# Strassen pairs in the first feed-forward as in the second, with both start-ups reordered

## What is computed

```python
x = rms_norm(x, final_norm_w)                                   # end of the first block: x's own norm
x = x + 0.5 * swiglu_ffn(rmsnorm(x, ffn1_norm), ffn1_w_in, ffn1_w_down)
...
mem_n = rmsnorm(mem, mem_norm)                                  # the memory's norm
x = x + 0.5 * swiglu_ffn(rmsnorm(x, ffn2_norm), ffn2_w_in, ffn2_w_down)

def swiglu_ffn(x, w_in, w_down):
    a, b = jnp.split(x @ w_in, 2, axis=-1)                      # w_in is 1024 x 5632
    return (jax.nn.silu(a) * b) @ w_down                        # w_down is 2816 x 1024
```

## Time and profile before

| | |
|---|---|
| median of 3 runs | 2434.7 us (2434.04 to 2436.02) |
| the profiled execution's own time | 2434.53 us |
| its span | 2432.8 us |
| PE busy | 2409.9 us, 99% of the span |
| DVE, ACT, POOL busy | 1243.0, 1095.1, 1314.3 us |
| granted TensorE clock, mean of the span | 0.997 of full speed |
| DMA | 92 GB/s mean |
| chain that ended last | PE 90%, DVE 7%, ACT 2% |

### The profile page before, as it was taken

The page is one execution under the profiler, slowest core; times in us unless marked ns, Lnnn a source line. Parts: engine busy times, 40 slices in busy tenths (PEclk is TensorE's granted clock), DMA queues, the critical chain, the costliest instruction groups (busy, mean ns, idle before and its releaser), DMA issues.

```text
span 2432.8 us, 33977 instructions
## 1 busy us (share of the span) xinstructions
PE 2409.9 (99%) x13114; PEld 2014.6 (83%) x13114; DVE 1243.0 (51%) x2325; ACT 1095.1 (45%) x1686; POOL 1314.3 (54%) x1722
## 2 busy tenths in 40 slices
PE   9999999999999999999999999999999999899998
PEld 6887788888788787888888888878988788899987
DVE  7965765322796586432332113199366433766502
ACT  5444676323534467532443323242366523566521
POOL 5553544555564455455555554585443455777753
PEclk9999999999999999999999999999999999999999
DMA  4232221222222212222322232332222222233322
GB/s 150 91 120 77 70 78 66 99 96 96 86 96 75 87 61 79 78 96 96 113 96 96 97 101 89 128 117 78 79 85 71 70 95 95 87 105 105 105 96 87
DMA packets 64412, 224.45 MB, mean 92 GB/s; under 512 B 7367, under 2 KB 10951, under 8 KB 64124
## 3 DMA queue, kind: packets, MB, share of 16 engines
q1 hardware_dynamic: 62620, 216.49, 26.7%
q0 software_dynamic: 1632, 5.78, 0.8%
HBM read 219.57 MB, written 3.99 MB: 92 GB/s over the span
## 4 chain that ended last, share of the span: by engine, by line
PE 90%; DVE 7%; ACT 2%; issue 0%; DMA 0%; SPq 0%; DVEq 0%; ACTq 0%
PE proj L193 69%; PE proj L2144 5%; PE att L2144 3%; PE att L193 2%; PE proj L914 1%; PE att L893 1%; PE att L1005 1%; PE att L904 1%; PE att L992 1%; PE att L2344 1%; PE att L947 1%; PE att L936 1%; DVE h_low L551 1%; ACT b_logits L2793 1%; DVE dk L1466 0%; DVE probs L1497 0%
## 5 line engine op out<-in xcount | busy, mean ns | idle before, releaser
L170 POOL TENSOR_TENSOR weight_low<-ring,weight_high 128x256 fp32r<-128x256 f32 x1432 | 1120.5, 814 | 1002.9 <-ACT weight_high L140 980.5
L193 PE MATMUL proj<-h_high,weight_high 128*128 128x512 f32 x1648 | 647.9, 393 | 1.6 <-POOL weight_low L170 1.5
L193 PE MATMUL proj<-h_low,weight_high 128*128 128x512 f32 x1648 | 641.7, 389 | 0.0
L193 PE MATMUL proj<-h_high,weight_low 128*128 128x512 f32 x1648 | 641.6, 389 | 0.0
L140 ACT ACTIVATE weight_high<-ring 128x1024 fp32r<-128x1024 f32 x353 | 371.7, 1054 | 354.6 <-PE proj L193 323.0
L193 PEld LDWEIGHTS proj<-h_high,weight_high 128*128 128x128 f32 x1648 | 309.4, 188 | 71.3 <-issue 5.1
L193 PEld LDWEIGHTS proj<-h_low,weight_high 128*128 128x128 f32 x1648 | 309.3, 188 | 65.1
L193 PEld LDWEIGHTS proj<-h_high,weight_low 128*128 128x128 f32 x1648 | 309.5, 188 | 62.4
L193 PE MATMUL proj<-b_act_high,weight_high 128*128 128x512 f32 (+1 forms) x352 | 135.0, 383 | 0.0
L193 PE MATMUL proj<-b_act_high,weight_low 128*128 128x512 f32 (+1 forms) x352 | 134.7, 383 | 0.0
L193 PE MATMUL proj<-b_act_low,weight_high 128*128 128x512 f32 (+1 forms) x320 | 122.6, 383 | 0.0
(11 more groups left out here) (623 smaller groups left out, 4711.2 us busy)
## 6 DMA issues: line engine op xcount, KB each, us to landing
ring<-in_stream SPq DMA_DIRECT2D x398, 512.0 KB, 3.4
xT<-in_x SPq DMA_DIRECT2D x4, 512.0 KB, 6.9
idx<-gate_rows POOLq DMA_DIRECT2D x8, 256.0 KB, 4.2
out<-hT SPq DMA_DIRECT2D x8, 256.0 KB, 2.2
bias_rows<-bias_row SPq DMA_DIRECT2D x2, 512.0 KB
b_logits<-in_mem POOLq DMA_DIRECT2D x1, 1024.0 KB, 8.1
bias_rows<-bias_row SPq DMA_DIRECT2D x1, 768.0 KB
consts<-in_const SPq DMA_DIRECT2D x1, 576.0 KB, 10.4
```

Of the source, the lines that this page charges most:

```text
L170: self.s_low.on(pool.tensor_tensor(self.low[:, c % self.slots, cols], self.raw[:, c % self.slots, cols], self.high[:, c % HIGH, cols], ALU ...
L193: mm = pe.matmul(out, a, b, start=(k == 0 and i == 0), stop=(k == n - 1 and i == 2))
```

## The change

- `ffn1` is paired as `ffn2` is. Its leads are a0, b0, a1, b1; its steps 2 to 21 are pairs. The dense step, its silu, gating and splits are gone.
- In both, the norm's sum stands before the lead's sixth slice (k = 5, was k = 6), and its spread before the eighth (k = 7, was at b0's first).
- Both start-ups (from the spread to the end of pair 0) are reordered on DVE and ACT. The weight forms of pair 0 go to other banks (`form_banks`), so that they need not wait for the leads to be emptied. T2's raw form has a place of its own, which lets T2's low part go ahead of T4. T4's high part and a1's silu go behind the snapshots of pair 0. ACT's first two form highs change places. In pair 0 DVE makes the forms of pair 1 behind two of its corners.
- x's own norm is spread over the pairs: two squares in each of pairs 2 to 5, the sum on PE before pair 7 (in a bank of its own), the root in pair 7, half of the reciprocal in each of pairs 8 and 9, one tile scaled in each of pairs 10 to 17.
- The memory is loaded when the last pair's T1 corner is done; its squares follow on ACT in d0, and its sum and norm come behind d1 (was d0). `power_rows`, 64 small matmuls, moves from behind d3 to behind d5.

The diff, cut to its core:

```diff
 NORMS = ["0", "1", "ffn1", "mix", "ffn2", "fin2"]
-SPLIT_NORMS = NORMS[:4]
-PAIRED = ["f2"]
+SPLIT_NORMS = ["0", "1", "mix"]
+PAIRED, PAIRED_NORMS = ["f1", "f2"], ["ffn1", "ffn2"]
...
-    total, spread = ((2, 0), (2, 2)) if n == NORMS[0] else ((0, KD - 2), (1, 0))
+    total, spread = ((2, 0), (2, 2)) if n == NORMS[0] else ((0, 5), (0, 7)) if n in PAIRED_NORMS else ((0, KD - 2), (1, 0))
...
+X_TOTAL = 7
+X_SQUARES = {j: (2 * j - 4, 2 * j - 3) for j in range(2, 6)}
+X_INVERSE = {8: slice(0, HALF), 9: slice(HALF, T)}
+X_SCALE = 10
 HIGH_AT = {0: [], 1: [0, 1], 2: [2, 3], NP: [KF - 1]}
...
-        if n in PAIRED:
-            g += [(f"{n}a1", OWN), (f"{n}b1", OWN)] + [(f"{n}p{i}", OWN) for i in range(2, KF)]
-        for i in range(1, KF if n not in PAIRED else 1):
-            g += [(f"{n}a{i}", "a" if i > 1 else OWN), (f"{n}b{i}", "v")]
-            if n == "f1" and i == 7:
-                g += [("ms_x", "a")]
-        g += [(f"{n}d0", "v")] + between + [(f"{n}d{d}", "v") for d in range(1, KD)]
+        g = [(f"ms_{n}", "a")] + [(f"{n}{x}{i}", OWN) for i in range(2) for x in "ab"]
+        for j in range(NP):
+            g += [("ms_x", OWN)] if n == "f1" and j == X_TOTAL else []
+            g += [(f"{n}p{j + 2}", OWN)]
...
+    def form_banks(n, j):
+
+        return (att[4], att[5], pair_alpha(n, 1)) if j == 0 else att[0:3]
     def s_slot(z):
...
             for j in range(NP):
+                if n == "f1" and j == X_TOTAL:
+                    G.open(pe, "ms_x")
+                    pe.wait_ge(s_xsum.sem, 1)
...
                     continue
                 product(f"{n}d{d}", xs, ready)
-                if n == "f1" and d == 0:
+                if n == "f1" and d == 1:
                     memory_sum()
-                if n == "f1" and d == 3:
+                if n == "f1" and d == 5:
                     power_rows()
...
+        def memory():
+
+            W.round(act, "f1d0")
+            act.wait_ge(s_mem.sem, 16)
+            for k in range(KD):
+                s_msq.on(act.activation(memsq[:, k, :], memT[:, k, :], ACT.Square))
...
+            act.wait_ge(s_sf.sem, s_sf.base + 2 * q_ + 1)
+            W.used(act, cb - HIGH)
+            s_sh.on(act.activation(W.high[:, cb % HIGH, 0:T], b1[:, :], ACT.Copy))
             act.wait_ge(s_sf.sem, s_sf.base + 2 * q_ + 2)
             s_slot_free(act, 3 * q_)
-            s_sh.on(act.activation(s_slot(3 * q_)[0], att[1][:, :], ACT.Copy))
-            W.used(act, cb - HIGH)
-            s_sh.on(act.activation(W.high[:, cb % HIGH, 0:T], att[0][:, :], ACT.Copy))
+            s_sh.on(act.activation(s_slot(3 * q_)[0], b2[:, :], ACT.Copy))
             act.wait_ge(s_sf3.sem, s_sf3.base + 2 * q_ + 2)
             s_sh.on(act.activation(s_slot(3 * q_ + 1)[0], s_slot(3 * q_ + 1)[2], ACT.Copy))
...
             at = KD * NORMS.index(norm)
             act.wait_ge(S.s_h.sem, at + 4)
-            x_high_part("11")
-            act.wait_ge(s_tf.sem, s_tf.base + 1)
-            x_high_part("T1")
-            W.round_one(act)
+            x_high_part(n, "11")
+            act.wait_ge(s_tf.sem, formed + 1)
+            x_high_part(n, "T1")
             act.wait_ge(S.s_h.sem, at + KD)
             norm_copy(S, act, norm)
-            x_high_part("21")
+            x_high_part(n, "21")
+            act.wait_ge(s_tf.sem, formed + 2)
+            x_high_part(n, "T2")
+            W.round_one(act)
             act.preload_act_table_set("silu_and_others")
-            act.wait_ge(s_tf.sem, s_tf.base + 2)
-            x_high_part("T2")
             act.wait_ge(s_lead.sem, base + 1)
             s_silu.on(act.activation(act_raw(0), act_raw(0), ACT.Silu))
-            x_high_part("22")
             form_highs(n, 0)
-            act.wait_ge(s_tf.sem, s_tf.base + 4)
-            x_high_part("T3")
-            act.wait_ge(s_lead.sem, base + 3)
-            s_silu.on(act.activation(act_raw(1), act_raw(1), ACT.Silu))
-            G.whole(act, f"{n}b1")
-            x_high_part("T4")
+            x_high_part(n, "22")
+            act.wait_ge(s_tf.sem, formed + 3)
+            x_high_part(n, "T3")
             for j in range(NP):
                 if j + 1 < NP:
                     W.round_one(act)
                 snapshots(n, j, lambda: gate_highs(j))
+                if j == 0:
+                    act.wait_ge(s_tf.sem, formed + 4)
+                    G.whole(act, f"{n}b1")
+                    x_high_part(n, "T4")
+                    act.wait_ge(s_lead.sem, base + 3)
+                    s_silu.on(act.activation(act_raw(1), act_raw(1), ACT.Silu))
+                if n == "f1" and j in X_SQUARES:
+                    for k in X_SQUARES[j]:
+                        s_xsq.on(act.activation(x_squares[:, k, :], xT[:, k, :], ACT.Square))
+                if n == "f1" and j == X_TOTAL:
+                    G.whole(act, "ms_x")
...
-            s_sf.on(dve.tensor_tensor(att[1][:, :], att[0][:, :], a[:, 0:T], ALU.subtract))
+            s_sf.on(dve.tensor_tensor(b2[:, :], b1[:, :], a[:, 0:T], ALU.subtract))
             settle(dve, s_sf)
-            s_sf.on(dve.tensor_tensor(att[2][:, :], a[:, T:UNIT], att[1][:, :], ALU.subtract))
+            s_sf.on(dve.tensor_tensor(b4[:, :], a[:, T:UNIT], b2[:, :], ALU.subtract))
...
+            s_tf.on(dve.tensor_tensor(x_form(n, "T1"), x_form(n, "12"), x_form(n, "11"), ALU.subtract))
             for k in range(4, KD):
                 scaled(k)
             settle(dve, s_tf)
             settle(dve, S.s_h)
-            s_tf.on(dve.tensor_tensor(T_raw["T2"], B_raw["22"], T_raw["T1"], ALU.subtract))
+            s_tf.on(dve.tensor_tensor(x_form(n, "T2"), x_form(n, "22"), x_form(n, "T1"), ALU.subtract))
+            t_low("T1")
             dve.wait_ge(S.s_copied.sem, copied)
             G.whole(dve, f"{n}a0")
             s_lead.on(dve.tensor_tensor(act_raw(0), att[0][:, :], rstd[:], ALU.mult))
+            weight_forms(n, 0)
+            form_low(n, 0, 0)
+            t_low("T2")
+            form_low(n, 0, 1)
+            s_tf.on(dve.tensor_tensor(x_form(n, "T3"), x_form(n, "22"), x_form(n, "12"), ALU.subtract))
             G.whole(dve, f"{n}b0")
             link(dve.tensor_tensor(att[1][:, :], att[1][:, :], rstd[:], ALU.mult))
-            t_low("T1")
-            dve.wait_ge(s_silu.sem, base // 3 * 2 + 1)
+            t_low("T3")
+            form_low(n, 0, 2)
+            dve.wait_ge(s_xpl.sem, s_xpl.base + 12 * f + 4)
+            s_tf.on(dve.tensor_tensor(x_form(n, "T4"), x_form(n, "21"), x_form(n, "T2"), ALU.subtract))
+            dve.wait_ge(s_silu.sem, 2 * f + 1)
             s_lead.on(dve.tensor_tensor(act_raw(0), att[1][:, :], act_raw(0), ALU.mult))
+            t_low("T4")
             G.whole(dve, f"{n}a1")
             s_lead.on(dve.tensor_tensor(act_raw(1), att[2][:, :], rstd[:], ALU.mult))
-            settle(dve, s_lead)
-            weight_forms(n, 0)
-            form_low(n, 0, 0)
-            dve.wait_ge(s_xpl.sem, s_xpl.base + 4)
-            settle(dve, s_tf)
-            s_tf.on(dve.tensor_tensor(T_raw["T4"], B_raw["21"], T_raw["T2"], ALU.subtract))
-            t_low("T2")
-            form_low(n, 0, 1)
-            s_tf.on(dve.tensor_tensor(T_raw["T3"], B_raw["22"], B12, ALU.subtract))
-            t_low("T3")
-            form_low(n, 0, 2)
-            t_low("T4")
             for j in range(NP):
                 more = j + 1 < NP
                 if j >= 1:
...
                 gate_lows(j)
+                if n == "f1":
+                    own_norm(j)
+                if j == 0:
+                    corner(n, j, 0)
+                    corner(n, j, 1)
+                    weight_forms(n, j + 1)
+                    corner(n, j, 2)
+                    for m in range(3):
+                        form_low(n, j + 1, m)
+                    continue
...
+        def own_norm(j):
+
+            for k in X_SQUARES.get(j - 1, ()):
+                dve.wait_ge(s_xsq.sem, k + 1)
+                if k >= 1:
+                    ins = dve.tensor_tensor(x_rstd, x_squares[:, 0, :] if k == 1 else x_rstd, x_squares[:, k, :], ALU.add)
+                    if k < KD - 1:
+                        link(ins)
+                    else:
+                        s_xsum.on(ins)
+            if j in X_INVERSE:
+                dve.wait_ge(s_xroot.sem, s_xroot.base + 1)
+                link(dve.reciprocal(x_rstd[:, X_INVERSE[j]], x_rstd[:, X_INVERSE[j]]))
+            k = j - X_SCALE
+            if 0 <= k < KD:
+                s_xscale.on(dve.scalar_tensor_tensor(xT[:, k, :], xT[:, k, :], vec("fin1", k), x_rstd, ALU.mult, ALU.mult))
+
         def half_sum(i):
...
-        s_mem.on(pool.dma_start(memT, A["mem"]), 16)
...
+        pool_pairs("f1")
+        pool.wait_ge(s_product.sem, s_product.base + 6 * pair_of("f1", NP - 1) + 2)
+        s_mem.on(pool.dma_start(memT, A["mem"]), 16)
+        W.rest(pool, f"f1d{KD - 1}")
```

239 lines of the change are left out of this document (77 added, 162 removed).

## The result

The changed kernel took **2421.57 us** (median of 4, 2421.04 to 2422.23) beside 2434.43 us before (median of 4, 2434.04 to 2436.02): ratio 0.9948, 95% interval 0.9936 to 0.9960, so 12.9 us faster. The profiled execution took 2421.36 us with a span of 2419.3 us and a mean granted clock of 0.998. The forecast was 2419.5 us in a range of 2415 to 2427.5.

What follows compares the result with a forecast made beforehand. PE, busy for 99% of the span, was taken as the bound. Pairs 16.0, less norms 0.6, less `ffn1`'s new start-up 4.2, plus 8.07 - 4.2 for `ffn2`'s, gave 15.1 us: 2419.5 us, range 2415 to 2427.5.

Steps and rivals of the forecast that it cites:

- Pairs, 16.0: In `ffn1`, twenty dense steps of 10.88 us become twenty pairs of 10.08, taking 16.0 us off PE's path.
- Norms, 0.6: In both feed-forwards' leads, moving the norm's sum and spread up costs PE 0.6 us in all.
- cost: 0.3 us on PE in each feed-forward: At the norm's sum, moved behind 15 lead matmuls, PE waits some 0.3 us for DVE.
- Start-up, 4.2 each: Each feed-forward's beginning loses 4.2 us (8.07 before), POOL's 22 pieces from 15.6 on letting pair 1 begin at 38.2.
- x's own norm, 0: In `ffn1`'s pairs, the spread squares, additions, root, reciprocal and scaling cost 0; PE's sum is one matmul as before.
- hidden with 0.3 to spare: In pair 7, ACT's 3.25 us of table loads and root delay the next first snapshot to 12.6; PE wants it by 12.96.
- Memory, 0: Around d0 to d5, the memory's load, squares, norm and `power_rows` cost 0, none having been on PE's path.
- Clock, whole: In both start-ups the granted clock stays at 1.00 through PE's gaps of some 1 to 2 us each.
- Strict exclusion of DVE and POOL: Start-up rival: all 8.7 us of DVE work blocks POOL; pair 1 at 40.2, loss 6.2 each, 2423.5 us; chance 0.12.
- the floor: Start-up rival: POOL is not the last wait, DVE sets a loss of 2.5 each, 2416 us; chance 0.10.
- no wait in pairs 7 to 18: Sign expected in the new profile: PE does not wait in pairs 7 to 18.
- no pair over 10.2: Sign in `ffn1`: pairs 10.08 us apart; any pair over 10.2 would show the prediction wrong.

Runs made afterwards that it cites:

- e6_form3: Changed kernel with POOL making pair 0's third form ahead of block 21's low part, not behind it: 2421.58 us.
- e7_snap: Changed kernel with ACT's first snapshot of pair 0 ahead of T3's high part and the next chunk's: 2422.46 us.
- e11_norm: Changed kernel with the norm's sum and spread back at their old places among the leads' matmuls: 2419.37 us.
- e5_relief: Changed kernel with the low part of block 22 made by DVE in one piece instead of by POOL in four: 2421.93 us.
- e1_corner: Changed kernel with DVE writing corner 1 ahead of the next pair's first form's low part in pair 7 of `ffn1`: 2420.77 us.
- e2_root: Changed kernel with the table loads and root of x's own norm moved into ACT's waits for PE in pair 7: 2419.85 us.
- e3_nonorm: Changed kernel with x's own norm left out of the first feed-forward: 2418.55 us.
- e10_b: Changed kernel with block 22's low part on DVE, root in ACT's gaps, POOL, DVE reordered, pair 1's first two forms ahead of T4's low part: 2418.20 us.

## Why the prediction came out as it did

The direction, the main term and the last wait of the start-ups were right; the total was 2.1 us too good, with errors in both directions.

- **Pairs, 16.0: right.** 10.08 us a pair in `ffn1` as in `ffn2`, 0.12 us a matmul. The estimate from the figure of the Trainium skill ("TensorE: Matmul & The Clock Gate", "Wait — 56ns, not 53.3ns?") was 9.17 us a pair; the trace does not agree.
- **Norms, 0.6: the step "cost: 0.3 us on PE in each feed-forward" failed twice.** On PE it measured 0.55 and 0.43 (24.18 and 24.06 against 23.63). And the move cost POOL 1.0 more in each by the chunk's release, which I did not follow: with it undone pair 1 starts 1.1 and 1.0 earlier. I had counted it as a gain of 0.35 to the start-up; DVE's scaling did begin earlier, but by 0.24 (7.22 behind the first lead matmul, 7.46 before), and with no gain at pair 1.
- **Start-up, 4.2 each: mis-sized, it measured 5.0.** POOL was named rightly as the last wait, and e6_form3 and e7_snap show that T2's gap is slack. The sum put pair 1 at 38.2; it stood at 39.1. The term that failed is the place from which POOL's 22 pieces were counted, 15.6: the low parts of block "21" began at 16.7 (2074.30 in `ffn2`), and in e11_norm at 15.98, where they had begun before. The price of the pieces was nearly right, 22.4 us here and 22.1 in e11_norm against 22.6. So the missing 1.0 is the norm's; that e11_norm's pair 1 stands at 38.1, the forecast's place to 0.1, is in part luck, since its start is 0.4 later and its pieces are 0.5 cheaper than in the sum. What I did not see is a second chain through DVE of nearly the same length (e5_relief), which in turn waited 2.0 for POOL's fourth form. T2's gap was 1.9 where I had 1.0, because of that wait, and cost nothing.
- **x's own norm, 0: wrong by 1.25.** The step "hidden with 0.3 to spare" compared ACT's high parts with the next pair's first snapshot alone, and that one was in time. It did not ask what DVE had queued behind its wait for those high parts: corner 1 of the pair in hand. That is 1.45 in pair 7 (e1_corner and e2_root give back 1.20 and 1.45). The sum on PE fell from 1.05 (before, the next matmul started 0.94 behind it and the one after that 0.11 late) to 0.85 us, near the forecast "as before". All the rest is free (e3_nonorm).
- **Memory, 0: right**, with the load faster than assumed. That the lags' wait of 1.3 us would go I had not counted.
- **Clock, whole: wrong in `ffn1`** (0.76), right in `ffn2`, and worth nothing in this kernel, since both pairs 0 last 15.0. The step that failed took a gap of 1.25 us as the measure for one that came out at 1.9. In e10_b, with less waiting behind the fall, it did cost, 0.75.
- **Rivals.** Strict exclusion of DVE and POOL put pair 1 at 40.2, the floor at 36.5; measured 39.1, of which 1.0 is another cause. As a sum exclusion was too dear; as a mechanism it is close to what the rows show (last section). Of the marks set out beforehand, "no wait in pairs 7 to 18" failed in pair 7, "no pair over 10.2" in pairs 6 and 7, and the clock row in `ffn1`; pair 0 took 15.0 and not 14.3.

The errors: 1.7 for the start-ups (10.1 against 8.4), 1.25 for x's own norm (2.30 in pairs 6 and 7 less the 1.05 of before), 0.4 for the leads, together 3.3 too good; against them 1.7 in stretches that I had put at zero, of which 1.5 is variation between executions and 0.24 the change. That leaves 1.6: 13.5 of span in place of 15.1. The 1.5 is luck: on the two feed-forwards alone the sum was 3.3 too good.

## What to carry to other kernels

When a step is moved earlier on the engine that bounds, ask which buffer's release it now stands in front of: here a 1 us norm inside a product held back a cast, that cast a GpSimd queue, and that queue the start of the next stage, for more than three times the price booked (2.2 us against 0.6). Where an engine is said to be late but "in time" for its reader, look at what the reader's engine has queued behind that wait, for other readers. And when relief of the engine that the wait names gives nothing, look for a second chain of nearly equal length before giving up the theory: two edits worth nothing each were worth 2.4 us together.

## What was unexpected in the hardware

The clock's fall was not the same for the same gap. With 1.90 or 1.91 us of idle PE ahead of T2 in both feed-forwards, the granted clock fell to 0.76 in `ffn1` and stayed at 1.00 in `ffn2` of the changed kernel, and did the reverse in e5_relief. With the same gaps it fell in neither in e1_corner (1.00 from 1234 to 1241 and from 2087 to 2094) and in both in e2_root (0.84 and 0.82 there). A share of 0.76 is a mean: in `ffn1` of the changed kernel the matmuls of corner "21" were 0.21 us apart, the lower level (1.2 GHz), and from 1236.8 on 0.12 again. The windows of e5_relief, `ffn1` and then `ffn2`:

```profile
1233.00:1240.00 7.00, 5.80 (x49) 5.63 (x48) 6.44 (x9) 2.08 (x3) 5.63 (x4) 1.00 0.25 78
...
2087.00:2094.00 7.00, 7.00 (x48) 7.00 (x47) 6.48 (x9) 2.07 (x3) 6.08 (x5) 0.76 0.27 66
```

DVE and POOL slow each other both ways. The subtraction that makes T2's raw form, the same instruction on the same data, took 1.74 us in the changed kernel, where POOL works beside it, and 1.23 us in e11_norm, where POOL stood idle from 2071.14 to 2072.74:

```profile
2071.99 1.74 DVE L3073 TENSOR_TENSOR b_big<-b_qkvx,b_x_T 128x1024 f32<-128x1024 f32 x1
```

```profile
2071.18 1.23 DVE L3073 TENSOR_TENSOR b_big<-b_qkvx,b_x_T 128x1024 f32<-128x1024 f32 x1
```

The prediction had let only POOL pay for that. POOL's pieces beside that subtraction in the changed kernel show how the two share: the one under way when it began took 0.74 us, as it does alone, and the next 1.73.

```profile
2071.92 0.74 POOL L3517 TENSOR_TENSOR b_x_low<-b_qkvx,b_x_high 128x256 fp32r<-128x256 f32 x1
...
2072.61 1.73 POOL L3517 TENSOR_TENSOR b_x_low<-b_qkvx,b_x_high 128x256 fp32r<-128x256 f32 x1
```

So the subtraction is 0.51 longer, no more than what was left of the piece under way (to 2072.66), and the next piece 1.0 longer, about what was then left of the subtraction (to 2073.73): they take turns. The Trainium skill ("SBUF — State Buffer", "SBUF: two separate sides") has the one that starts first block the other for the whole length of its instruction; here the trace agrees to some 0.15 us.
